# Final norm and stores of all rows moved ahead of the last expert block's output, whose rows are gathered, summed, normed and scattered afterwards

## The chip, the cores and the metric

One core of one Trainium2 chip runs the whole program in one launch. The metric is device time in microseconds (us), from the start of the program to its end. The time before is the median of three runs.

## The reference, cut to what matters

Two transformer blocks work on 1024 tokens of 1024 float32 features. The first is left out here: the change doesn't touch it. The second ends in a mixture of 32 experts, two per token, and a final norm:

```python
def second_block(x, ...):
    ...
    x = x + gate_a * mix
    h = rms_norm_2(x, norm2_g[l]) * (1.0 + scale_f) + shift_f
    x = x + gate_f * hierarchical_moe(h, ...)
    return rms_norm_2(x, final_g)

def rms_norm_2(x, g):                       # over the 1024 features of a token
    y = x * lax.rsqrt(jnp.mean(x * x, axis=-1, keepdims=True) + EPS)
    return y * g

# hierarchical_moe: each token goes to 2 of 32 experts (d_model 1024, hidden 512)
#   y[token] += gate[token, e] * ((silu(h @ w_gate[e]) * (h @ w_up[e])) @ w_down[e])
```

## The kernel before

**Expert blocks.** Tokens are sorted into blocks of 128 slots. Blocks 0 to 31 are the first 128 tokens of each expert. An expert with more tokens gets overflow blocks (32, 33, ...), whose number is known only on the chip; with these inputs there are four (32 to 35), so block 35 is the last. A slot without a token has the index 1024, which the bounds check of the indirect DMAs skips. `h4_dram` holds the inputs of the experts and `x3_dram` the residual stream, to which every block adds its gated output with an accumulating indirect DMA (a scatter, `scatter_rows`, line 838, on the GpSimd queue).

**One overflow block** (`overflow(b)` of each engine) streams twelve chunks of weights of 512 KB through a ring of twelve slots (`ring`, SyncE, line 595). ScalarE rounds each chunk to fp32r (`mH`, line 1338), VectorE makes the remainder (`mL`, line 2095), and TensorE forms each product from three fp32r matmuls (lines 2139, 2140, 2142). Eight chunks are gate and up, four are down. Between these two groups TensorE transposes the gathered inputs of the next block (2634) and the hidden rows (2639), which VectorE (2101, 2105, 2110) and ScalarE (1341, 1345) prepare. At chunk 6 of block b, the output of the block before it is taken from PSUM (banks 4 and 5): ScalarE weights it by slot (`slot_w`) into `ys[1]` (line 1331), GpSimd waits until VectorE has made all twelve remainders, copies the destination indices (904), multiplies by the gate row (`gate_rows`, line 832) and scatters (838).

**The loop around it** (`overflow_blocks`, lines 421 to 429) runs over all 15 possible overflow blocks on each engine, with an `If` on the count read from the chip: the eleven that don't exist are empty turns of compare and branch.

**After the last block** ScalarE takes its output from PSUM in two halves (1353), GpSimd gates them (832) and scatters them into `x3_dram` (838, `last_tok`). When that scatter has landed, SyncE loads all eight tiles of 128 rows back from `x3_dram` (602). For each tile ScalarE sums the squares (1358), VectorE forms mean plus epsilon (`variance`, 2117), GpSimd raises it to the power -0.5 (923), VectorE multiplies by it and by `final_row` (`finish`, 2122), and SyncE stores the tile to `out` (605). The program ends when all stores have landed.

Of the kernel before, what the change touches and what calls it, by code (L numbers as in the profile page):

```python
# [12 lines left out]
P = 128  # L13
# [22 lines left out]
    tr_lo sums_out sums2_out sums_in row_cols row_tr row_copied rows_out rows_here c_here mid_tr tr_mid v_mm pool_steps neg_out mb_in mask_done exp_done small_ready small_exp sq_out intra_out kt_mm kw_out st_mm c_ready hd_out cell_w ov_l last_y last_out m2_row m2_dst rows_known aff_ready halves_out affT_tr m1_xT_lo m1_hid m1_hT_lo if_lo v_odd if_mm pool_mm k_mm k_out s_mm  # L36
# [47 lines left out]
def build(nc, ctx, io, out, room):  # L84
# [159 lines left out]
    for name in SEMS.split():  # L244
# [6 lines left out]
        [("sq2", NT), ("sq2_2", NT), ("sq_final", NT)],  # L251
        [("var2", NT), ("var2_2", NT), ("var_final", NT)],
        [("rstd2", NT), ("rstd2_2", NT), ("rstd_final", NT)],
# [166 lines left out]

    def overflow_blocks(eng, overflow):
# [10 lines left out]
    one_rows = [ring[:, 2 * t, :] for t in range(6)] + [xz[:, 6, :], sg]  # L432
    two_rows = [ring[:, 2 * t + 1, :] for t in range(6)] + [xz[:, 7, :], hid]
    x_rows = [(mH, mL)[t // WSETS][:, t % WSETS, :].bitcast(F32) for t in range(NT)]
# [16 lines left out]
    def _(sp):  # L451
# [145 lines left out]
        overflow_blocks(sp, overflow)  # L597

        sp.wait_ge(S["last_out"], 16)  # L600
        for t in range(NT):
            sp.dma_start(x_rows[t], x3_tiles[:, t, :]).then_inc(x_in[t], 16)
        for t in range(NT):
            sp.wait_ge(S["final_done"], t + 1)
            sp.dma_start(out.rearrange("(t p) d -> p t d", p=P)[:, t, :], one_rows[t]).then_inc(x_in[t], 16)
# [5 lines left out]
    def _(pool):  # L611
# [279 lines left out]
        def overflow(b):  # L891
# [7 lines left out]
            pool.wait_ge(m2_out[1], 16 * (E2 // 2 - 1) + XS_PAST)  # L899
            pool.wait_ge(m2_out[0], 16 * b + 16 * (E2 // 2) + XS_PAST)  # L900
            settle(pool)
            pool.wait_ge(S["m2_lo"], 12 * b + 12 * E2 + 11 + past["m2_lo"])
            settle(pool)
            pool.tensor_copy(tok_out[0][:], row_of[:, bass.ds(b + (E2 - 1), 1)]).then_inc(S["m2_row"], 1)
            gate_rows(gated, ys[1], slice(0, D))
            pool.wait_ge(S["m2_row"], 2 * b + 3 * (E2 - 1) + 2)
            settle(pool)
# [3 lines left out]
        pool.wait_ge(m2_out[1], 16 * (E2 // 2 - 1) + XS_PAST)  # L911
        pool.wait_ge(m2_out[0], 16 * blocks + 16 * (E2 // 2) + XS_PAST)
        settle(pool)
        pool.tensor_copy(last_tok[:], row_of[:, bass.ds(blocks + (E2 - 1), 1)]).then_inc(S["m2_row"], 1)
# [3 lines left out]
        pool.wait_ge(S["m2_row"], 2 * blocks + 3 * (E2 - 1) + 3)  # L918
        settle(pool)
        scatter_rows(ys[0], last_tok).then_inc(S["last_out"], 16)  # L920
        for t in range(NT):
            pool.wait_ge(S["var_final"], t + 1 + past["var_final"])
            pool.tensor_tensor(stat[:, 10, t:t + 1], stat[:, 9, t:t + 1], neghalf[:, 0:1], ALU.pow).then_inc(S["rstd_final"], 1)
# [3 lines left out]
    def _(act):  # L927
# [395 lines left out]
        def overflow(b):  # L1323
            used, hi = past["m2_used"] + 12 * E2, past["m2_xT_hi"] + 2 * E2
            for c in range(12):
                if c == 6:
                    act.wait_ge(S["m2_used"], 12 * b + used)
# [1357 lines left out]
```

## Time and profile before

| | us |
|---|---|
| time before, median of three runs | 2220.2 |
| the three runs | 2221.27, 2218.15, 2220.2 |
| span of the profiled execution, first to last instruction | 2217.8 |
| last matmul ends | 2183.1 |
| last scatter into x3_dram issued | 2188.5 |
| first reload of x3_dram issued | 2193.5 |
| last tile normed | 2212.0 |

The profile gives no time of its own for the profiled execution beside the span, which is 2.4 us below the median of the runs. TensorE is busy for 91% of the span, VectorE for 76%, ScalarE for 57%, GpSimd for 21%. All times of rows are microseconds from the start of the span. A name with a "q" behind the engine (POOLq) is its instruction queue, in which branches and the issue of DMAs run.

### The profile page before, as it was taken

The numbers are of one execution on the slowest core, as the hardware profiler recorded it, in microseconds if no ns is written. First come the engines' busy times: TensorE is split into PE (matmuls) and PEld (weight loads), VectorE is DVE, ScalarE is ACT, GpSimd is POOL, SyncE is SP. The second block draws the span as 40 slices with busy tenths as digits, with TensorE's granted clock in tenths as the row PEclk, the third lists the DMA queues.
The fourth block names the chain that finished last, engine by engine and source line by source line (L and its number), as shares of the span: only waits on it lengthen the run. The fifth ranks groups of instructions, "written<-read, shape, count | busy, mean of one in ns | idle before, by whom it ended". The sixth has DMA issues, their size and how long they took to land.

```text
span 2217.8 us, 31469 instructions
## 1 busy us (share of the span) xinstructions
PE 2018.8 (91%) x9493; PEld 1669.2 (75%) x9493; DVE 1695.3 (76%) x1917; ACT 1257.1 (57%) x1478; POOL 470.0 (21%) x371
## 2 busy tenths in 40 slices
PE   3999999959999999999599998975999999999993
PEld 3888878747888887878477776864888888788872
DVE  5676765469999999999517455446999999999994
ACT  4311112108888878787515423214888888888874
POOL 2000001101001011110101450110444443334533
PEclk9999999959999999999799999987999999999997
DMA  9276844629999999999411103354999999999994
GB/s 346 89 250 223 270 169 158 218 76 349 387 381 385 382 378 389 380 387 382 161 39 48 48 20 117 123 206 152 386 388 375 382 379 378 365 376 382 342 363 162
DMA packets 236193, 598.33 MB, mean 270 GB/s; under 512 B 24513, under 2 KB 61653, under 8 KB 236125
## 3 DMA queue, kind: packets, MB, share of 16 engines
q1 hardware_dynamic: 209536, 524.35, 63.5%
q0 software_dynamic: 22928, 60.93, 9.4%
q10 hardware_dynamic: 3660, 12.17, 1.5%
q8 instruction: 39, 0.64, 0.1%
q14 instruction: 30, 0.24, 0.0%
HBM read 567.39 MB, written 51.43 MB: 279 GB/s over the span
## 4 chain that ended last, share of the span: by engine, by line
PE 63%; DMA 14%; DVE 10%; SPq 4%; issue 4%; ACT 3%; POOL 1%; DVEq 0%; ACTq 0%; POOLq 0%
PE ps L2139 19%; PE ps L2142 18%; PE ps L2140 18%; DMA ring<-in_w_expert_up 6%; DMA ring<-in_moe_w_down 6%; SPq L533 4%; DVE mL L1630 1%; PE ps L2267 1%; DMA ring<-in_ada_w 1%; PE ps L2562 1%; PE ps L2407 1%; DVE mL L2026 1%; DVE xz L1776 1%; PE ps L2232 1%; ACT mH L1276 1%
## 5 line engine op out<-in xcount | busy, mean ns | idle before, releaser
L2026 DVE TENSOR_TENSOR mL<-ring,mH 128x1024 fp32r<-128x1024 f32 x384 | 482.9, 1299 | 17.6 <-ACT mH L1276 17.0
L1630 DVE TENSOR_TENSOR mL<-ring,mH 128x1024 fp32r<-128x1024 f32 x384 | 455.4, 1221 | 31.6 <-ACT mH L1095 22.0
L1095 ACT ACTIVATE mH<-ring 128x1024 fp32r<-128x1024 f32 x384 | 402.3, 1063 | 96.2 <-PE ps L2142 64.6
L2139 PE MATMUL ps<-mH,xsH 128*128 128x512 f32 x1088 | 437.1, 402 | 7.8 <-DVE mL L2026 4.4
L1276 ACT ACTIVATE mH<-ring 128x1024 fp32r<-128x1024 f32 x384 | 397.6, 1057 | 57.8 <-DMA ring<-in_w_expert_up 24.0
L2142 PE MATMUL ps<-mH,xsL 128*128 128x512 f32 x1088 | 427.4, 393 | 0.0
L2140 PE MATMUL ps<-mL,xsH 128*128 128x512 f32 x1088 | 425.7, 391 | 0.0
L2139 PEld LDWEIGHTS ps<-mH,xsH 128*128 128x128 f32 x1088 | 205.9, 189 | 48.9 <-issue 7.3
L2142 PEld LDWEIGHTS ps<-mH,xsL 128*128 128x128 f32 x1088 | 205.3, 189 | 44.4
L2140 PEld LDWEIGHTS ps<-mL,xsH 128*128 128x128 f32 x1088 | 206.0, 189 | 39.7
L2139 PE MATMUL ps<-mH,hidH 128*128 128x512 f32 x544 | 216.3, 398 | 9.1 <-DVE hidL L1675 5.7
L832 POOL TENSOR_TENSOR xz<-xz,gate_ffn_row 128x340 f32<-128x340 f32 (+3 forms) x99 | 166.8, 1690 | 247.8 <-DVE mL L2026 210.2
L2140 PE MATMUL ps<-mL,hidH 128*128 128x512 f32 x544 | 212.3, 390 | 0.0
L2142 PE MATMUL ps<-mH,hidL 128*128 128x512 f32 x544 | 167.9, 390 | 0.0
L2139 PE MATMUL ps<-hH,wH 128*128 128x512 f32 x384 | 152.1, 396 | 3.7 <-DVE hL L1432 3.3
L2140 PE MATMUL ps<-hL,wH 128*128 128x512 f32 x384 | 150.4, 392 | 0.0
L2139 PEld LDWEIGHTS ps<-mH,hidH 128*128 128x128 f32 x544 | 102.2, 188 | 33.6 <-DVE mL L1630 8.8
L1376 DVE SCALAR_TENSOR_TENSOR acc<-ring,silu_c,acc 128x1024 f32<-128x1024 f32 x83 | 106.6, 1284 | 21.7 <-DMA ring<-in_ada_w 14.8
L2142 PE MATMUL ps<-hH,wL 128*128 128x512 f32 x384 | 122.9, 391 | 0.0
L2142 PEld LDWEIGHTS ps<-mH,hidL 128*128 128x128 f32 x544 | 102.2, 188 | 21.8
L2140 PEld LDWEIGHTS ps<-mL,hidH 128*128 128x128 f32 x544 | 102.4, 188 | 19.7
L703 POOL DMA_INDIRECT xz<-h_dram,tok_in x16 | 37.1, 2322 | 376.0 <-DVE tok_in L1640 376.0
(419 smaller groups left out, 3162.7 us busy)
## 6 DMA issues: line engine op xcount, KB each, us to landing
ring<-in_w_expert_gate SPq DMA_DIRECT2D x144, 512.0 KB, 12.7
ring<-in_w_expert_up SPq DMA_DIRECT2D x144, 512.0 KB, 12.8
ring<-in_w_expert_down SPq DMA_DIRECT2D x144, 512.0 KB, 13.0
ring<-in_moe_w_gate SPq DMA_DIRECT2D x128, 512.0 KB, 11.7
ring<-in_moe_w_up SPq DMA_DIRECT2D x128, 512.0 KB, 11.6
ring<-in_moe_w_down SPq DMA_DIRECT2D x128, 512.0 KB, 13.7
ring<-in_ada_w SPq DMA_DIRECT2D x96, 512.0 KB, 7.0
ring<-in_sc_w_in SPq DMA_DIRECT2D x24, 512.0 KB, 8.8
```

The costliest lines, as they stand in the source:

```text
L533: sp.dma_start(dst, src).then_inc(ring_in[s], 16)
L703: pool.indirect_dma_start(out=xs[r], out_offset=None, in_=h2_dram, in_offset=bass.IndirectOffsetOnAxis(ap=tok_in[r][:, 0:1], axis=0)).then ...
L832: pool.tensor_tensor(dst[:, at], src[:, at], gate_ffn_row[:, at], ALU.mult).then_inc(S["m2_row"], 1)
L1095: act.activation(mH[:, m % WSETS, :], ring[:, m % RING, :], ACT.Copy).then_inc(S["m1_hi"], 1)
L1276: act.activation(mH[:, wset, :], ring[:, slot, :], ACT.Copy).then_inc(S["m2_hi"], 1)
L1376: ins = dve.scalar_tensor_tensor(out=acc[:], in0=slot, scalar=silu_c[:, silu_col + k:silu_col + k + 1], in1=acc[:], op0=ALU.mult, op1=ALU.add)
L1630: dve.tensor_tensor(mL[:, m % WSETS, :], ring[:, m % RING, :], mH[:, m % WSETS, :].bitcast(F32), ALU.subtract).then_inc(S["m1_lo"], 1)
L1776: ins = dve.scalar_tensor_tensor(out=xz[:, i, back:T], in0=tA[:, 0:T - back], scalar=col("conv_w_2", 4 * (3 - back) + i), in1=xz[:, i, bac ...
L2026: dve.tensor_tensor(mL[:, wset, :], ring[:, slot, :], mH[:, wset, :].bitcast(F32), ALU.subtract).then_inc(S["m2_lo"], 1)
L2139: pe.matmul(o, high, rh, start=start, stop=False)
L2140: pe.matmul(o, high, rl, start=False, stop=False)
L2142: last = pe.matmul(o, low, rh, start=False, stop=stop)
```

## The change

The rows of all tiles are reloaded once the output of the last block but one has been scattered, into ring slots as VectorE frees them, and normed and stored without the last block's contribution. That contribution is handled apart, in `ys[0]`: GpSimd gathers its tokens' rows from `x3_dram`; VectorE takes the last block's output from PSUM, weighted and gated in one operation (`weigh`), and adds the gathered rows; the sum is normed as a ninth tile (sixth in order, `FINAL_ORDER`) and scattered over `out` when all eight stores have landed. In the overflow blocks, `weigh` on VectorE takes the place of ScalarE's copy and GpSimd's multiplication, and GpSimd no longer waits for VectorE's remainders before the scatter.

```diff
+    FINAL_ORDER = [0, 1, 2, 3, 4, NT, 5, 6, 7]
+    x_rows = [ring[:, t, :] for t in range(NT)]
+    sq_rows = [ring[:, NT + u, :] for u in range(RING - NT)]
+    last_rows, last_base = ys[0], xz[:, 7, :]
 # SyncE, after the overflow blocks
-        sp.wait_ge(S["last_out"], 16)
+        sp.wait_ge(m2_out[0], 16 * (E2 // 2) + XS_PAST)
+        sp.wait_ge(m2_out[1], 16 * blocks + 16 * (E2 // 2 - 1) + XS_PAST)
         for t in range(NT):
+            sp.wait_ge(S["m2_lo"], 12 * blocks + 12 * (E2 - 1) + t + 1 + past["m2_lo"])
             sp.dma_start(x_rows[t], x3_tiles[:, t, :]).then_inc(x_in[t], 16)
         for t in range(NT):
             sp.wait_ge(S["final_done"], t + 1)
-            sp.dma_start(out...[:, t, :], one_rows[t]).then_inc(x_in[t], 16)
+            sp.dma_start(out...[:, t, :], x_rows[t]).then_inc(x_in[t], 16)
 # GpSimd, overflow(b)
             pool.wait_ge(S["ov_y"], b + 1 + past["ov_y"])
-            pool.wait_ge(S["m2_lo"], 12 * b + 12 * E2 + 11 + past["m2_lo"])
-            pool.tensor_copy(tok_out[0][:], row_of[...]).then_inc(S["m2_row"], 1)
-            gate_rows(gated, ys[1], slice(0, D))
-            scatter_rows(gated, tok_out[0]).then_inc(m2_out[0], 16)
+            pool.tensor_copy(tok_out[1][:], row_of[...]).then_inc(S["m2_row"], 1)
+            scatter_rows(ys[1], tok_out[1]).then_inc(m2_out[1], 16)
 # GpSimd, after the overflow blocks
-        for half in range(2):
-            pool.wait_ge(S["last_y"], half + 1)
-            gate_rows(ys[0], ys[0], slice(512 * half, 512 * half + 512))
-        scatter_rows(ys[0], last_tok).then_inc(S["last_out"], 16)
-        for t in range(NT):
-            ... pow of tile t
+        pool.indirect_dma_start(out=last_base, in_=x3_dram, in_offset=last_tok, ...).then_inc(S["last_in"], 16)
+        for i in range(NT + 1):
+            ... pow of entry i
+        for t in range(NT):
+            pool.wait_ge(x_in[t], 64)
+        pool.wait_ge(S["last_done"], 1)
+        pool.indirect_dma_start(out=out, in_=last_rows, out_offset=last_tok, ...).then_inc(S["last_out"], 16)
+        pool.wait_ge(S["last_out"], 16)
 # ScalarE: its copy at chunk 6 of overflow(b) and the two halves after the blocks are removed
-        for t in range(NT):
-            act.wait_ge(x_in[t], 48)
-            act.activation(two_rows[t], x_rows[t], ACT.Square, accum_out=...)
+        act.wait_ge(S["m2_lo"], 12 * blocks + 12 * E2 + past["m2_lo"])
+        for i, t in enumerate(FINAL_ORDER):
+            act.wait_ge(x_in[t], 48) if t < NT else act.wait_ge(S["last_y"], 1)
+            act.activation(sq_rows[i % 4], x_rows[t] if t < NT else last_rows, ACT.Square, accum_out=...)
 # VectorE
+        def weigh(dst, block):
+            return dve.scalar_tensor_tensor(out=dst, in0=ps[:, 4:6, :], scalar=slot_w[:, bass.ds(block, 1)],
+                                            in1=gate_ffn_row, op0=ALU.mult, op1=ALU.mult)
         def overflow(b):
             for c in range(12):
+                if c == 6:
+                    dve.wait_ge(S["m2_used"], 12 * b + 12 * E2 + past["m2_used"])
+                    dve.wait_ge(m2_out[1], 16 * b + 16 * (E2 // 2 - 1) + XS_PAST)
+                    weigh(ys[1], b + (E2 - 1)).then_inc(S["ov_y"], 1)
+        def last_sum():
+            dve.wait_ge(S["m2_used"], 12 * blocks + 12 * E2 + past["m2_used"])
+            step(weigh(last_rows, blocks + (E2 - 1)))
+            dve.wait_ge(S["last_in"], 16)
+            dve.tensor_tensor(last_rows, last_rows, last_base, ALU.add).then_inc(S["last_y"], 1)
-        for t in range(NT):
-            variance(t)
-            if t:
-                finish(t - 1)
-        finish(NT - 1)
+        for i, t in enumerate(FINAL_ORDER):
+            if t == NT:
+                last_sum()
+            variance(i)
+            if i:
+                finish(i - 1)
+        finish(NT)
```

## Rows read from the trace of the kernel before

**Rows 1.** Timeline of TensorE: start us, us, engine line operation; the last matmuls.
```profile
2182.01 0.39 PE L2139 MATMUL ps<-mH,hidH 128*128 128x512 f32 x1
2182.24 0.39 PE L2140 MATMUL ps<-mL,hidH 128*128 128x512 f32 x1
2182.47 0.61 PE L2142 MATMUL ps<-mH,hidL 128*128 128x512 f32 x2
```

**Rows 2.** Timeline of GpSimd after the last block; idle before a row in brackets.
```profile
2178.03 1.61 POOL L838 DMA_INDIRECT x_dram<-xz,tok_out  x1 [0.89 <-POOL xz L832]
2184.99 0.18 POOL L914 COPY last_tok<-row_of 128x1 uint32 x1 [5.36 <-DMA x_dram<-xz,tok_out]
2185.14 2.48 POOL L832 TENSOR_TENSOR xz<-xz,gate_ffn_row 128x512 f32<-128x512 f32 x2
2188.51 1.60 POOL L838 DMA_INDIRECT x_dram<-xz,last_tok  x1 [0.90 <-POOL xz L832]
```

**Rows 3.** Timeline of SyncE's queue: reloads, then stores.
```profile
2193.53 2.75 SPq L602 DMA_DIRECT2D mH<-x_dram  x6
...
2210.87 1.53 SPq L605 DMA_DIRECT2D out<-xz  x2
```

**Rows 4.** Timeline of ScalarE: end of the blocks, then the squares.
```profile
2176.78 1.10 ACT L1345 ACTIVATE xsH<-ps 128x512 fp32r<-128x512 f32 x2
2183.30 1.26 ACT L1353 ACTIVATE xz<-ps,slot_w 128x512 f32<-128x512 f32 x2 [5.42 <-PE ps L2142]
2196.86 1.06 ACT L1358 ACTIVATE ring<-mH 128x1024 f32<-128x1024 f32 x1 [12.30 <-DMA mH<-x_dram]
...
2200.62 1.06 ACT L1358 ACTIVATE ring<-mH 128x1024 f32<-128x1024 f32 x1 [0.89 <-DMA mH<-x_dram]
...
2201.90 1.06 ACT L1358 ACTIVATE ring<-mH 128x1024 f32<-128x1024 f32 x1
```

**Rows 5.** Timeline of VectorE: norms of the last tiles.
```profile
2206.57 1.28 DVE L2122 SCALAR_TENSOR_TENSOR ring<-mH,stat,final_row 128x1024 f32<-128x1024 f32 x1 [0.38 <-POOL stat L923]
...
2207.84 1.27 DVE L2122 SCALAR_TENSOR_TENSOR ring<-mH,stat,final_row 128x1024 f32<-128x1024 f32 x1
...
2209.55 2.48 DVE L2122 SCALAR_TENSOR_TENSOR xz<-mL,stat,final_row 128x1024 f32<-128x1024 f32 x2 [0.38 <-POOL stat L923]
```

**Rows 6.** DMA issues: size, median us from issue to landing; last row whole trace, others the end.
```profile
mH<-x_dram SPq DMA_DIRECT2D x6, 512.0 KB, 6.6
...
mL<-x_dram SPq DMA_DIRECT2D x2, 512.0 KB, 10.1
out<-xz SPq DMA_DIRECT2D x2, 512.0 KB, 5.3
...
x_dram<-xz,last_tok POOLq DMA_INDIRECT x1, 5.0
...
x_dram<-xt POOLq DMA_DIRECT2D x16, 512.0 KB, 2.9
```

**Rows 7.** DMA issues of four narrow windows: 2193.5, 2159.4, 2161.3 and 2124.2 us.
```profile
mH<-x_dram SPq DMA_DIRECT2D x1, 512.0 KB, 3.3
...
x_dram<-xz,tok_out POOLq DMA_INDIRECT x1, 6.0
...
xz<-h_dram,otok POOLq DMA_INDIRECT x1, 4.2
...
xz<-h_dram,otok POOLq DMA_INDIRECT x1, 7.9
```

**Rows 8.** Branches of the loop over overflow blocks: count, ns min/median/max, first and last start.
```profile
L427 ACTq COMPARE_BRANCH  x15: 39/50/55, 2100.8 to 2182.6; - x15
...
L427 POOLq COMPARE_BRANCH  x15: 39/50/55, 2108.2 to 2184.3; - x15
```

**Rows 9.** Timeline of VectorE in overflow blocks 32 and 35.
```profile
2103.80 15.09 DVE L2095 TENSOR_TENSOR mL<-ring,mH 128x1024 fp32r<-128x1024 f32 x12
2118.81 0.74 DVE L2101 TENSOR_TENSOR xz<-xz,ps 128x256 f32<-128x256 f32 x2
...
2160.04 6.91 DVE L2095 TENSOR_TENSOR mL<-ring,mH 128x1024 fp32r<-128x1024 f32 x6
2167.30 3.50 DVE L2095 TENSOR_TENSOR mL<-ring,mH 128x1024 fp32r<-128x1024 f32 x3 [0.35 <-ACT mH L1338]
2171.27 3.50 DVE L2095 TENSOR_TENSOR mL<-ring,mH 128x1024 fp32r<-128x1024 f32 x3 [0.48 <-ACT mH L1338]
2175.21 0.75 DVE L2101 TENSOR_TENSOR xz<-xz,ps 128x256 f32<-128x256 f32 x2 [0.44 <-PE ps L2142]
```

**Rows 10.** Line 1652 of the first block's experts: count, ns min/median/max, first and last start.
```profile
L1652 DVE SCALAR_TENSOR_TENSOR xz<-ps,slot_gate,gate_ffn_row x16: 1273/1274/1278, 541.8 to 1064.3; 128x1024 f32<-128x1024 f32 x16
```

**Rows 11.** Timeline: VectorE's first remainder of block 32; GpSimd's copy and scatter there.
```profile
2103.80 1.88 DVE L2095 TENSOR_TENSOR mL<-ring,mH 128x1024 fp32r<-128x1024 f32 x1
...
2118.01 0.92 POOL L904 COPY tok_out<-row_of 128x1 uint32 x1 [7.26 <-DVE mL L2095]
...
2122.28 1.60 POOL L838 DMA_INDIRECT x_dram<-xz,tok_out  x1 [1.01 <-issue]
```

More of the change, by code:

```diff
@@ L419, in m2_steps, with stat_of @@
             body(s // 2, s % 2)
+    FINAL_ORDER = [0, 1, 2, 3, 4, NT, 5, 6, 7]
+    def stat_of(i):
+        return [stat[:, 8 + n, i:i + 1] if i < NT else stat[:, 11, n:n + 1] for n in range(3)]
     def overflow_blocks(eng, overflow):
@@ L604, in _ @@
             sp.wait_ge(S["final_done"], t + 1)
-            sp.dma_start(out.rearrange("(t p) d -> p t d", p=P)[:, t, :], one_rows[t]).then_inc(x_in[t], 16)
+            sp.dma_start(out.rearrange("(t p) d -> p t d", p=P)[:, t, :], x_rows[t]).then_inc(x_in[t], 16)
         for t in range(NT):
@@ new lines, in _ @@
+        for i in range(NT + 1):
+            pool.wait_ge(S["var_final"], i + 1 + past["var_final"])
+            own = stat_of(i)
+            pool.tensor_tensor(own[2], own[1], neghalf[:, 0:1], ALU.pow).then_inc(S["rstd_final"], 1)
+        for t in range(NT):
+            pool.wait_ge(x_in[t], 64)
+        pool.wait_ge(S["last_done"], 1)
+        pool.indirect_dma_start(out=out, in_=last_rows, in_offset=None,
+                                out_offset=bass.IndirectOffsetOnAxis(ap=last_tok[:, 0:1], axis=0),
+                                bounds_check=T - 1, oob_is_err=False).then_inc(S["last_out"], 16)
@@ L2087, in _ @@
         m2_steps(dve, m2_step)
+        def weigh(dst, block):
+            return dve.scalar_tensor_tensor(out=dst.rearrange("p (a b) -> p a b", a=2), in0=ps[:, 4:6, :],
+                                            scalar=slot_w[:, bass.ds(block, 1)],
+                                            in1=gate_ffn_row[:].rearrange("p (a b) -> p a b", a=2),
+                                            op0=ALU.mult, op1=ALU.mult)
         def overflow(b):
@@ L2111, in overflow, with variance, finish @@
                                   part.bitcast(F32), ALU.subtract).then_inc(S["m2_xT_lo"], 1)
-        overflow_blocks(dve, overflow)
-        def variance(t):
-            dve.wait_ge(S["sq_final"], t + 1 + past["sq_final"])
-            dve.tensor_scalar(stat[:, 9, t:t + 1], stat[:, 8, t:t + 1], 1.0 / D, EPS, ALU.mult,
-                              ALU.add).then_inc(S["var_final"], 1)
-        def finish(t):
-            dve.wait_ge(S["rstd_final"], t + 1 + past["rstd_final"])
-            dve.scalar_tensor_tensor(out=one_rows[t], in0=x_rows[t], scalar=stat[:, 10, t:t + 1], in1=final_row[:],
-                                     op0=ALU.mult, op1=ALU.mult).then_inc(S["final_done"], 1)
-        dve.wait_ge(S["final_in"], 16)
-        for t in range(NT):
-            variance(t)
-            if t:
-                finish(t - 1)
-        finish(NT - 1)
+        blocks = overflow_blocks(dve, overflow)
+        def last_sum():
+            dve.wait_ge(S["m2_used"], 12 * blocks + 12 * E2 + past["m2_used"])
+            settle(dve)
+            dve.wait_ge(m2_out[0], 16 * (E2 // 2) + XS_PAST)
+            step(weigh(last_rows, blocks + (E2 - 1)))
+            dve.wait_ge(S["last_in"], 16)
+            dve.tensor_tensor(last_rows, last_rows, last_base, ALU.add).then_inc(S["last_y"], 1)
+        def variance(i):
+            own = stat_of(i)
+            dve.wait_ge(S["sq_final"], i + 1 + past["sq_final"])
+            dve.tensor_scalar(own[1], own[0], 1.0 / D, EPS, ALU.mult, ALU.add).then_inc(S["var_final"], 1)
+        def finish(i):
+            t = FINAL_ORDER[i]
+            own, rows = stat_of(i), x_rows[t] if t < NT else last_rows
+            dve.wait_ge(S["rstd_final"], i + 1 + past["rstd_final"])
+            dve.scalar_tensor_tensor(out=rows, in0=rows, scalar=own[2], in1=final_row[:], op0=ALU.mult, op1=ALU.mult
+                                     ).then_inc(S["final_done" if t < NT else "last_done"], 1)
+        dve.wait_ge(S["final_in"], 16)
+        for i, t in enumerate(FINAL_ORDER):
[5 more added lines that the diff above has]
+        finish(NT)
     @block.tensor
```

59 lines of the change are left out of this document (26 added, 33 removed).

## The prediction

> **What bounds the kernel now.** I read the page's chain of work that ended last for the whole, then one timeline per engine after 2090 us, then the landings of DMAs. Up to 2183.1 us the chain is TensorE's and the change only touches its overflow blocks. The tail from the last matmul [rows 1] to the end of the span at 2217.8 is 34.7 us in which nothing is multiplied. The reader should see it as a relay. ScalarE takes the product (two halves, 1.26), GpSimd, held by earlier work until 2184.99, gates it (2.48) and issues the scatter 0.90 later at 2188.51 [rows 2, 4]; this lands after 5.0 [rows 6], and the first reload goes out at 2193.53 [rows 3]. That is 10.4 us from matmul to reload. The first tile lands 3.3 later [rows 7]. Then squares, powers and norms follow each other, and the last norm ends at 2212.03 [rows 5]; its store is issued at once, lands 5.3 later [rows 3, 6], and 0.4 later the span ends.
>
> Two more things matter. The norm pipeline isn't bound by ScalarE, whose squares go 1.28 apart [rows 4]: VectorE's `finish` starts 1.27, then 1.71 after the last one, in turn [rows 5], since every second power waits on GpSimd. So a tile costs 1.49. And after the last real block each engine walks through eleven empty turns: ScalarE's last product ends at 2177.88 and its last turn branches at 2182.6, GpSimd goes from its scatter at 2178.03 to 2184.3 [rows 2, 4, 8]. With the instructions that follow, ScalarE is free at about 2183.0 and GpSimd about 6.8 us after its last scatter.
>
> **The overflow blocks.** `weigh` doesn't occur in this stage, but line 1652 is the same operation with the same shapes and operands in PSUM and SBUF: 1.274 us [rows 10]. Two such in a row start 1.20 apart (2.48 for two [rows 5]), so it lengthens VectorE's stream by 1.20. In block 32 VectorE works through twelve remainders without a gap and goes straight into the hidden rows that TensorE waits for [rows 9]: here 1.2 is added to the path. In blocks 33 to 35 the same stream has gaps of 0.35, 0.48 and 0.44, 1.27 in all [rows 9]. They hide the 1.20, the more so as ScalarE loses its copy of 1.1 us in front of chunk 6, so the rounded chunk is there earlier. I take nothing for these three; if the cover is gone it is 1.2 each, 3.6. What ScalarE and GpSimd lose (the copy, a gate multiplication and a wait) hides behind other work now and gives nothing back. So the last matmul moves from 2183.1 to **2184.3**, and ScalarE is free from its turns at 2183.0 + 1.2 = 2184.2.
>
> **The reloads.** The scatter of block 34 used to go out at 2178.03. Now `weigh` in block 35 starts after six remainders, at 2166.95 + 1.2 = 2168.1, and ends at 2169.4. GpSimd copies the indices; such a copy took 0.92 beside VectorE's remainders [rows 11], and after it 0.9 pass until the DMA [rows 2]. The scatter starts at 2171.3, lands 6.0 later as its like did [rows 7], and the first reload goes out at 2177.4. SyncE's own turns are long over by then. The tiles land from 2180.7 on (3.3, 5.0, 7.1 after the first issue by the starts of the first three squares [rows 4], the last after some 13.4, which is 10.1 from its own issue [rows 6]). The waits on `m2_lo` cost nothing: the last ring slot needed is free at about 2172. So at 2184.3 two or more tiles are there and the others stay ahead of ScalarE by 1 to 3 us: it's not the reloads but ScalarE's empty turns that release the first square, 12.6 us sooner than at 2196.86. **No square falls in the last block's matmuls**; only the reloads do.
>
> **The norms.** Squares at 2184.3, 2185.6, 2186.8, 2188.1 and 2189.4. `finish(0)` follows `variance(1)`, at 2186.95; then 1.71, 1.27, 1.71: `finish(3)` runs from 2191.6 to 2192.85. Here the order is written out: `last_sum` comes next, with everything of VectorE behind it. Product and gather are long ready (GpSimd: scatter at 2171.3, turns until 2178.1, gather issued at 2180, landed in 4.2 alone to 7.9 beside streaming [rows 7], by 2188). `weigh` 1.25 and its own completion 0.1, add 1.2: 2195.4. ScalarE has stood idle since 2190.7; its sixth square ends at 2196.7. `variance(5)`, then `finish(4)` at 2196.8, and four more at steps of 1.71, 1.27, 1.71, 1.2: the last starts at 2202.7 and ends at **2203.9**, 8.1 us before the old 2212.03. Of the 12.6 gained at the first square the detour through `last_sum` takes 3.9 (`finish(4)` at 2196.8 instead of 2192.9) and the ninth row 1.5; 1.0 comes back since the second and third tile no longer wait for their loads.
>
> **The end.** New behind the last norm is the chain store, wait, scatter. The store: 5.3 for the last two before [rows 6], with reloads and stores back to back; alone a store of that size took 2.9 and a reload 3.3 [rows 6, 7]. After `last_sum` there is a gap of 5 us in the norms, and the stores drain, so I take 3.3 (bounds 2.9 and 5.3): landed at 2207.3. Then 0.9 from release to issue (0.3 to 1.0), 2208.2. Scatters to `x3_dram` took 5.0, this very list of rows, to 6.1; a gather of the kind, which moves rows without adding, 4.2. A plain write of rows isn't shown. I take 4.5 (bounds 4.0 and 6.1): 2212.7. With 0.4 the span ends at **2213.1**, 4.7 us sooner. On the median that is 2220.2 - 4.7 = **2215.5**.
>
> **Rivals.**
>
> *The stores stay slow.* The last store lands after 5.3 and the scatter after 6.1. For it: these are what the rows of the tail show. Against: those stores ran behind 4 MB of reloads. It gives +2.0 + 1.6: 2219.1, no change.
>
> *GpSimd's scatter is held up by VectorE.* The scatter of block 34 moves from a time when VectorE is nearly through into its unbroken stream. If it couldn't be issued until that stream ends, at 2176.2 instead of 2171.3, the reloads would start 4.9 later, the third tile would land at 2189.4 instead of 2184.5, and its square, due at 2186.8, and all behind it would be 2.6 late: 2218.1. Against: a scatter issued just as VectorE's stream began took 1.60 like those beside an idle VectorE [rows 2, 11]. The Trainium skill speaks for this in SBUF — State Buffer, section "SBUF: two separate sides", box "The 'DVE blocks DMA' trap": while VectorE runs an operation that holds the port pair it shares with GpSimd, GpSimd can't write the descriptors of its DMAs. By that rule, if the remainders count as such, the result is this rival's; by the rows it is the sum above.
>
> *VectorE becomes the bound of every overflow block.* The gaps sum to 1.27 against 1.20 added, a margin of 0.07. If they can't be used, and a remainder is stretched from 1.14 to 1.88 by GpSimd's copy, as the first one of block 32 was [rows 11], blocks 33 to 35 cost 1.94 each: +5.8, 2221.3, slower than before. The sign turns at 4.7 / 3 = 1.6 us per block, a loss of 0.2% needs 3.0. Against: the copy is 128x1 and ends at once when the port is free.
>
> **How the numbers follow.** About 0.2%, 4.4 us, is what can be told from no change here; the line lies at 2215.8, just beside my sum. The forecast as worked out, give or take 1.5: 0.52, a little over half of it below the line. Slow stores and scatter, whole or in part: 0.20. VectorE in the way of the scatter: 0.08. VectorE as the bound: 0.08. Better than the sum (store 2.9, scatter 4.0, release 0.3, which is 1.5 less: 2214.0): 0.12, nearly all faster. That makes faster 0.43, same 0.51, slower 0.06. The range goes from 2213.0 (the good bounds and 1.0 for a cheaper block 32) to 2221.0; the likeliest case's own is 2214.0 to 2217.0.
>
> **What would show it.** Step by step: remainders and `weigh` of block 32 end at about 2120.1 and the blocks after it stay 18.8 apart; first reload near 2177.4; first square at 2184.3 with idle time ended by no DMA; a gap of 4.6 on ScalarE after five squares; last norm near 2204; last store landing within 3.5; last scatter landing within 5. A first square later than 2186, a block longer than 19.5, or more than 10 us from the last norm to the end would make the prediction wrong.

## The result, and the profile after

The changed kernel takes 2224.57 us (2222.48 to 2227.02, 18 runs) against 2219.65 us (2216.39 to 2221.61, 18 runs) beside it. The ratio is 1.0022, with an interval of 1.0015 to 1.0029: slower by 4.9 us, where 4.7 us faster was forecast. A second set of runs of the same kernel (`e11`, below) gave 1.0021 (1.0012 to 1.0030). The time lies outside the range given, 2213.0 to 2221.0.

The profiled execution took 2223.24 us with a span of 2221.6 us, 3.8 us longer than the span of before. The granted clock is 0.958 over the whole. The blocks ahead of the change run 0.44 us earlier than in the execution of before, which is chance.

VectorE of the changed kernel in block 32, and again around block 35 (timeline: start, us, engine, line, operation):

```profile
2103.36 8.28 DVE L2112 TENSOR_TENSOR mL<-ring,mH 128x1024 fp32r<-128x1024 f32 x6
2111.56 1.27 DVE L2097 SCALAR_TENSOR_TENSOR xz<-ps,slot_w,gate_ffn_row 128x1024 f32<-128x1024 f32 x1
2112.76 6.89 DVE L2112 TENSOR_TENSOR mL<-ring,mH 128x1024 fp32r<-128x1024 f32 x6
...
2167.67 1.28 DVE L2097 SCALAR_TENSOR_TENSOR xz<-ps,slot_w,gate_ffn_row 128x1024 f32<-128x1024 f32 x1
2168.86 6.90 DVE L2112 TENSOR_TENSOR mL<-ring,mH 128x1024 fp32r<-128x1024 f32 x6
```

`weigh` takes 1.27 and stands between six remainders and six. From one block's copy of `otok` to the next's, block 32 lasts 19.66 us (before 18.46), blocks 33 and 34 last 18.79 and 18.88 (before 18.79 and 18.83). So the work in the blocks costs what was forecast: 1.2 once, nothing after. But look at the second half of block 35 beside [rows 9]: the gap of 0.48 that stood in it is gone, the six remainders follow each other without one.

GpSimd of the changed kernel, from block 35 to its last instruction:

```profile
2169.39 6.41 POOL L912 COPY tok_out<-row_of 128x1 uint32 x1 [6.39 <-DVE xz L2097]
2176.68 1.59 POOL L848 DMA_INDIRECT x_dram<-xz,tok_out  x1 [0.88 <-POOL tok_out L912]
2183.47 0.18 POOL L918 COPY last_tok<-row_of 128x1 uint32 x1 [5.19 <-issue]
2184.63 1.07 POOL L924 DMA_INDIRECT xz<-x_dram,last_tok  x1 [0.98 <-POOL last_tok L918]
...
2203.27 2.04 POOL L930 TENSOR_TENSOR stat<-stat,neghalf 128x1 f32<-128x1 f32 x2 [0.94 <-DVE stat L2143]
2211.02 1.05 POOL L934 DMA_INDIRECT out<-xz,last_tok  x1 [5.72 <-DMA out<-ring]
```

The first row is the surprise of the blocks: a copy of 128 words that takes 6.41 us. It starts at 2169.39 and ends at 2175.80; VectorE's six remainders end at 2175.76. The same copy took 6.40 in block 33 and 6.41 in block 34. The scatter behind it is 5.4 us later than forecast (2176.68 against 2171.3), and so is everything that waits for its landing.

SyncE's queue, then ScalarE's squares and VectorE's last norms:

```profile
2183.09 3.92 SPq L612 DMA_DIRECT2D ring<-x_dram  x8
2190.31 17.36 SPq L615 DMA_DIRECT2D out<-ring  x8
```

```profile
2186.49 1.06 ACT L1365 ACTIVATE ring<-ring 128x1024 f32<-128x1024 f32 x1 [7.78 <-DMA ring<-x_dram]
...
2190.34 1.06 ACT L1365 ACTIVATE ring<-ring 128x1024 f32<-128x1024 f32 x1 [1.44 <-DMA ring<-x_dram]
...
2198.87 1.06 ACT L1365 ACTIVATE ring<-xz 128x1024 f32<-128x1024 f32 x1 [4.14 <-DVE xz L2138]
```

```profile
2196.24 1.28 DVE L2097 SCALAR_TENSOR_TENSOR xz<-ps,slot_w,gate_ffn_row 128x1024 f32<-128x1024 f32 x1
2197.56 1.22 DVE L2138 TENSOR_TENSOR xz<-xz 128x1024 f32<-128x1024 f32 x1
...
2204.83 2.48 DVE L2149 SCALAR_TENSOR_TENSOR ring<-ring,stat,final_row 128x1024 f32<-128x1024 f32 x2 [0.38 <-POOL stat L930]
```

The last matmul ends at 2183.87 and the first reload goes out at 2183.09: only 0.8 us of what the change was to put beside the matmuls lies beside them. The idle time before the first square is ended by a load, and so is that before the third, fourth and fifth. The last norm ends at 2207.30, 4.7 before [rows 5], not 8.1. That is still sooner than before. What turns the sign comes later: the last store is issued at 2207.33 and lands 2.7 later, GpSimd's scatter starts at 2211.02 and lands after 2.9, at 2213.95, and yet the span ends at 2221.60.
```
kernel  engine   start us   lasts us
before  SyncE    2217.60    0.01
before  GpSimd   2209.22    8.02
after   SyncE    2210.29    0.01
after   GpSimd   2214.11    7.26
```

GpSimd's record ends the span of the changed kernel. In the kernel before it starts beside the last power (ended 2210.04), ends at 2217.24, 7.2 us after it, and lies hidden behind the last store with 0.4 us to spare.

The miss in the profiled execution, 2221.6 against 2213.1 forecast, is made up so: last norm +3.4, last store's landing -0.6 (2.7 for 3.3), release of the scatter +0.1, scatter's landing -1.6 (2.9 for 4.5), and from that landing to the end +7.2 (7.6 for 0.4). Sum +8.5.

### The profile page after: what moved, and what is told of

Its sections match the earlier page's. It is cut to its first block and busy times, and to the rows that moved or that the text cites. A ratio compares the mean times of both kernels' runs of the same rounds, so it can differ in the third digit from the quotient of the medians.

```text
span 2221.6 us, 31489 instructions
## 1 busy us (share of the span) xinstructions
PE 2014.1 (91%) x9493; PEld 1662.1 (75%) x9493; DVE 1700.7 (77%) x1925; ACT 1253.9 (56%) x1474; POOL 480.6 (22%) x367
## 5 line engine op out<-in xcount | busy, mean ns | idle before, releaser
L842 POOL TENSOR_TENSOR xz<-xz,gate_ffn_row 128x340 f32<-128x340 f32 (+1 forms) x93 | 155.3, 1674 | 249.1 <-DVE mL L2033 210.4
```

The lines of the kernel that those rows point to most:

```text
L842: pool.tensor_tensor(dst[:, at], src[:, at], gate_ffn_row[:, at], ALU.mult).then_inc(S["m2_row"], 1)
```

## The experiments

Each ratio is to the kernel before, run on the same chip beside it; its 95% interval is in brackets. The differences in us are those of the medians, unless a span is named.

### The end: is it GpSimd's last instruction?

`e3` is the kernel before with one thing added: after its last power GpSimd waits for all output stores.

```diff
             pool.tensor_tensor(stat[:, 10, t:t + 1], stat[:, 9, t:t + 1], neghalf[:, 0:1], ALU.pow)...
+        for t in range(NT):
+            pool.wait_ge(x_in[t], 64)
```

> Change of the kernel before: GpSimd, whose last power ends at 2210.0, also waits for the landing of all eight stores, at 2217.4; nothing else. Theory C (a drain of 7.2 us behind GpSimd's last instruction, hidden in the kernel before because it ends 0.4 us ahead of the last store's landing): 7 us slower than the kernel before. Rival D (the long drain belongs to the scatter into the output): no change, at most 0.3 us.

Measured: 2227.50 against 2220.72, 1.0028 (1.0017 to 1.0040), slower by 6.8 us. SyncE's stores of this kernel go out as in [rows 3], 0.7 later:

```profile
2201.22 8.97 SPq L605 DMA_DIRECT2D out<-ring  x6
2211.59 1.53 SPq L605 DMA_DIRECT2D out<-xz  x2
```

SyncE is through at 2218.42. GpSimd's DRAIN starts at 2218.44, lasts 7.18, and ends at 2225.62, 0.2 before the span's end at 2225.85. Nothing else was added, and the medians of the timed runs show 6.8. So GpSimd needs some 7.2 us after its last instruction or wait, and a kernel that lets it wait for the last transfer pays that.

`e2` takes the other way, in the changed kernel: SyncE, not GpSimd, waits for the landing of the last scatter.

```diff
-        pool.wait_ge(S["last_out"], 16)
 # SyncE, after its waits for the stores
+        sp.wait_ge(S["last_out"], 16)
```

> Change of the kernel after: GpSimd issues the last scatter and has nothing more to wait for; SyncE waits for its landing. Theory C (GpSimd takes some 7.2 us to drain once its last instruction is done, whatever that is): the drain starts 1.9 us sooner, beside the scatter's flight, 1.9 us faster. Rival D (the drain waits for the landing of the outstanding scatter and its length follows from that): no change, or a drain of over 9 us.

Measured: 2222.06 against 2220.72, 1.0008 (0.9999 to 1.0017), where the changed kernel has 1.0022 and 1.0021: 3.1 us less by the ratios, 3.6 by the medians, where 1.9 was expected. The two intervals together leave about 2.5 us either way, so 1.9 is not excluded.

```profile
2214.78 1.05 POOL L935 DMA_INDIRECT out<-xz,last_tok  x1 [5.72 <-DMA out<-ring]
```

The issue ends at 2215.83 and DRAIN at 2223.10, 7.27 later; the span ends 8.6 after the start of this row, in the changed kernel 10.6, so this trace shows 2.0. The landing of 2.9 us now lies beside the DRAIN, which is no longer for it. What is left, 7.3 from the end of the issue on, stands at the end of every version here in which GpSimd issues the last scatter.

### The scatter of block 34: its copy, or the port?

`e1` gives the copy of the indices to VectorE, in front of `weigh`; GpSimd only scatters.

```diff
 # GpSimd, overflow(b)
-            pool.tensor_copy(tok_out[1][:], row_of[:, bass.ds(b + (E2 - 1), 1)]).then_inc(S["m2_row"], 1)
-            pool.wait_ge(S["m2_row"], b + 3 * (E2 - 1) + 1)
+            pool.wait_ge(S["m2_dst"], b + E2)
 # VectorE, c == 6
+                    dve.tensor_copy(tok_out[1][:], row_of[...]).then_inc(S["m2_dst"], 1)
                     weigh(ys[1], b + (E2 - 1)).then_inc(S["ov_y"], 1)
```

> Change of the kernel after: VectorE, not GpSimd, copies the index column just ahead of weigh. Theory A (GpSimd's 128x1 copy waits 6.4 us for the port that VectorE's unbroken stream of remainders holds): the scatter of block 34 goes out at about 2170.2 instead of 2176.7, the first reload at 2176.4 instead of 2183.1, the first square at 2184 instead of 2186.5 (then ScalarE's empty turns hold it), the squares after it no longer wait for loads, the last norm ends at 2203.6 instead of 2207.3: 3.7 us faster than the kernel after. Rival B (the descriptors of the scatter are what VectorE's stream holds back, so the scatter waits with or without a copy): scatter still at 2176, no gain.

Measured: 2225.18 against 2220.72, 1.0020 (1.0011 to 1.0029): nothing gained. The copy is gone and the scatter itself has become long. VectorE, then GpSimd, of this kernel in block 35:

```profile
2171.12 1.27 DVE L2096 SCALAR_TENSOR_TENSOR xz<-ps,slot_w,gate_ffn_row 128x1024 f32<-128x1024 f32 x1
2172.31 6.89 DVE L2112 TENSOR_TENSOR mL<-ring,mH 128x1024 fp32r<-128x1024 f32 x6
```

```profile
2173.55 7.11 POOL L848 DMA_INDIRECT x_dram<-xz,tok_out  x1 [7.16 <-issue]
```

It starts 1.24 us into the remainders, which end at 2179.20, and it ends 1.46 after them, about what the whole instruction takes elsewhere (1.59). In blocks 32, 33 and 34 of this kernel the scatter took 5.73, 2.56 and 6.92: in block 33 it did not wait for the last remainder. The first reload leaves at 2185.49, 1.8 before the last matmul's end at 2187.28.

`e10` is `e1` with a hole in VectorE's stream: the remainder of chunk 7 computes a single column.

```diff
+                n = 1 if c == 7 else D
-                dve.tensor_tensor(mL[:, c % WSETS, :], ring[:, c, :], mH[:, c % WSETS, :].bitcast(F32),
+                dve.tensor_tensor(mL[:, c % WSETS, 0:n], ring[:, c, 0:n], mH[:, c % WSETS, 0:n].bitcast(F32),
```

> e1_copy_dve with VectorE's remainder of chunk 7 of each overflow block cut to one column (the other 1023 are stale, so the output is not the reference's): VectorE has about 1 us without work from 1.1 us after weigh on. Theory B (VectorE's unbroken stream of operations with two SBUF inputs keeps GpSimd from writing the descriptors of its scatter, and one gap is enough to let it in): the scatter of block 34 takes 1.6 to 3 us on GpSimd instead of 7.1, the first reload goes out 4 to 5 us sooner against the last matmul, and no square of the first five waits over 1 us for a load; kernel 2.5 to 4 us faster than e1_copy_dve. Rival N (the scatter is slow for its 128 rows and the weights streaming beside it): still 7 us.

Measured: 2219.84 against 2220.19, 0.9997 (0.9988 to 1.0006), 4.8 us less than `e1` by the differences. Not all of it is the scatter's: the last norm ends 19.8 after the last matmul, in `e1` 22.5, which is 2.7; block 32 is 1.1 shorter by the missing remainder (18.66 for 19.77); the rest may be the clock, which falls in `e1` (see `e7`) and not here. VectorE and GpSimd in block 35:

```profile
2169.09 2.57 DVE L2113 TENSOR_TENSOR mL<-ring,mH 128x1024 fp32r<-128x1024 f32 x3
2172.27 3.50 DVE L2113 TENSOR_TENSOR mL<-ring,mH 128x1024 fp32r<-128x1024 f32 x3 [0.61 <-ACT mH L1344]
```

```profile
2170.34 1.58 POOL L848 DMA_INDIRECT x_dram<-xz,tok_out  x1 [7.16 <-issue]
```

The same instruction takes 1.58 where a piece of the stream is missing: it starts before the next remainder does (2170.44). In block 34 it starts 0.1 into a whole remainder, takes 2.58, and ends 1.46 after that remainder, where the hole is. In block 32 it starts behind the hole, takes 4.96 and again ends 1.45 after the last remainder. In block 35 the scatter's rows and the weights that stream beside it are those of `e1`, so they aren't what made it slow there. The first reload leaves at 2176.76, 7.3 ahead of the last matmul's end at 2184.05, and no square waits for a load:

```profile
2184.64 1.06 ACT L1364 ACTIVATE ring<-ring 128x1024 f32<-128x1024 f32 x1 [5.76 <-issue]
...
2185.69 1.04 ACT L1364 ACTIVATE ring<-ring 128x1024 f32<-128x1024 f32 x1
```

This is the machine of the prediction: the square is released 5.76 after ScalarE's last product (2178.88) by nothing but its own empty turns. A hole was needed for that, so the kernel that computes everything doesn't have it.

The Trainium skill's rule that the prediction set against its rows (SBUF — State Buffer, "SBUF: two separate sides", the box "The 'DVE blocks DMA' trap") speaks of VectorE's operations in a 2-port mode. Block 35 behaves as it says, 7.11 with the stream and 1.58 with the hole, though the remainders are `tensor_tensor`. The same page, under "Who interferes with whom", infers that `tensor_tensor` doesn't hold up the writing of descriptors, since it takes only the read side of the pair. These runs show that it can hold up the issue of an indirect DMA; but that issue also takes its 128 indices from SBUF, and no run tells that reading from the writing of descriptors, so they don't refute the inference. The page also has the pair locked for one instruction; the traces agree with that in part.

Behind `weigh`, GpSimd's copy or scatter waited for the last of the remainders in 33 of 42 blocks (eleven kernels: all with `weigh` but `e10`), all eleven blocks 35 among them. In the other nine it got in when the one remainder that was running had ended (`e9`, block 33: 2.56, in a stream without a gap). And in front of `weigh` it always got in. The changed kernel, blocks 32 and 35:

```profile
2106.91 1.64 POOL L848 DMA_INDIRECT x_dram<-xz,tok_out  x1 [0.89 <-POOL xz L842]
2108.85 1.46 POOL L904 DMA_INDIRECT xz<-h_dram,otok  x1 [0.30 <-issue]
...
2161.71 1.29 POOL L904 DMA_INDIRECT xz<-h_dram,otok  x1 [2.11 <-DVE otok L2105]
```

VectorE's six remainders follow each other without a gap around all three (from 2103.36 and from 2160.85). So a hole lets the scatter in, but a stream without one doesn't always keep it out; what decides is open.

`e5` leaves out the scatters of the outputs of blocks 31 to 34, and the waits for them, so that the reloads wait for free ring slots alone. It shows the most that earlier reloads could bring.

```diff
-            scatter_rows(ys[1], tok_out[1]).then_inc(m2_out[1], 16)
```

> Change of the kernel after: the scatters of blocks 31 to 34 into x3_dram are left out (their contributions are missing from the output), and with them the waits on them; the index copies stay. The reloads then need only the ring slots. Theory A (late reloads hold the norms back by 3.4 us, and behind them stand ScalarE's eleven empty turns): reloads out by about 2172, all tiles there before ScalarE is free; first square 5.1 to 5.3 us after ScalarE's last product of block 35, five squares 1.28 apart with no wait for a DMA, last norm 19.6 us after the first square; 3 to 3.7 us faster than the kernel after. Rival E (something else than the reloads holds the first square, the turns being shorter or longer): first square as late as before, or earlier than 5.1 us after the last product.

Measured: 2222.30 against 2220.36, 1.0009 (1.0000 to 1.0018), 2.9 us less than the changed kernel by the ratios. The first reload leaves at 2167.57, the first square starts 5.8 after ScalarE's last product, and five squares follow 1.04 apart. The last norm ends 19.9 after the last matmul, in the changed kernel 23.4. Hence 3.5 us of the tail are the price of the late reloads, and so of the late scatter. (Its profiled execution has a fall of the clock in block 33, see `e7`; the tail is measured from the last matmul and so is free of it.)

### Both, and the order of the last rows

`e4` is `e1` and `e2` together.

> The first two edits together. Theories A and C: 3.7 + 1.9 = 5.6 us faster than the kernel after, 2219.0 against 2219.65 of the kernel before, no difference from it that can be measured. If B or D hold, one of the two parts is missing.

Measured: 2221.70 against 2220.72, 1.0007 (0.9998 to 1.0016), as `e2` alone: the copy's new place is worth nothing, as `e1` had said. The forecast above counted on more.

`e6` is `e4` with the detour moved: the tiles are squared and normed in the order 0 to 7, the last block's rows come ninth, and `last_sum` stands behind six finished tiles.

```diff
-    FINAL_ORDER = [0, 1, 2, 3, 4, NT, 5, 6, 7]
+    FINAL_ORDER = [0, 1, 2, 3, 4, 5, 6, 7, NT]
-            if t == NT:
+            if i == 7:
                 last_sum()
```

> e4_both with two edits: the last block's rows come last of the nine, and last_sum runs on VectorE ahead of the eighth variance. Theory F (last_sum with a wait on both sides costs 3.9 us in the sixth place, and as VectorE work alone 2.5; with the ninth rows last the last store lands under their norm): the gap of 4.4 us on ScalarE goes, the last norm ends about 1.3 us sooner against the first square, and the scatter follows it by 1 us plus what is left of the last store's flight instead of 3.6: 3 to 4 us faster than e4_both, and so 2 to 3 us faster than the kernel before. Rival G (the last norm is bound by the DMA transfers, not by the order): no gain over e4_both.

Measured: 2219.62 against 2220.36, 0.9998 (0.9989 to 1.0007), about 2 us less than `e4` (3 to 4 were expected, and the two traces show 3.0 from the last matmul on). The last norm is now that of the rows that no plain store takes away, so the last store is issued at 2203.54 and lands beside it; the scatter starts 2.7 after the last norm's end, not 3.7. The squares of tiles 5 to 7 no longer stand behind VectorE's sum either.

### The blocks

`e7` is the kernel before with the blocks' part of the change alone: `weigh` on VectorE, GpSimd's scatter right after it, no early reloads, norms as before.

```diff
-            pool.wait_ge(S["m2_lo"], 12 * b + 12 * E2 + 11 + past["m2_lo"])
-            gate_rows(gated, ys[1], slice(0, D))
-            scatter_rows(gated, tok_out[0]).then_inc(m2_out[0], 16)
+            scatter_rows(ys[1], tok_out[1]).then_inc(m2_out[1], 16)
 # ScalarE's copy at c == 6 is removed; VectorE, at c == 6, has the operation of weigh
+                    dve.scalar_tensor_tensor(out=ys[1]..., in0=ps[:, 4:6, :], scalar=slot_w[...],
+                                             in1=gate_ffn_row..., op0=ALU.mult, op1=ALU.mult)
```

> Change of the kernel before: only the overflow blocks' part of the change (weigh on VectorE at chunk 6, no gating and no wait for the remainders on GpSimd); the end is that of the kernel before. Theory H (1.2 us more in block 32, nothing in the three blocks after it): last matmul 1.3 us later against the start of block 32, whole kernel 0.3 to 1.3 us slower, since GpSimd was the last to be ready for the last output by 1.0. Rival I (VectorE is the bound of each block now): 4 to 5 us slower.

Measured: 2222.83 against 2220.36, 1.0009 (1.0000 to 1.0018), slower by 2.5, between the two theories. In its profiled execution block 32 lasts 20.00 and block 33 no less than 21.07, which neither had. The reason shows in TensorE's rows. `e2` has it too; there it is plainest. Busy times in block 33, in the changed kernel for the 6.6 us after the stall of block 32, in `e2` for the stall, 6.6 us of the slow stretch and 12 us behind it; columns: window, its length, then busy us (and count) of PE, PEld, DVE, ACT, POOL, then granted clock, DMA share, GB/s; first the changed kernel, then `e2`:

```profile
2121.60:2128.20 6.60, 6.60 (x29) 5.46 (x30) 6.45 (x9) 6.28 (x8) 1.98 (x2) 1.00 0.95 332
```

```profile
2117.70:2121.60 3.90, 2.25 (x13) 1.53 (x11) 3.90 (x5) 0.00 (x0) 1.60 (x1) 1.00 1.00 392
...
2123.40:2130.00 6.60, 6.60 (x17) 5.27 (x18) 5.02 (x8) 4.60 (x6) 1.27 (x1) 0.55 0.90 319
2130.00:2142.00 12.00, 12.00 (x55) 9.92 (x54) 11.32 (x10) 8.87 (x9) 2.42 (x2) 1.00 0.93 329
```

The granted clock falls from 2.4 to 1.2 GHz for 6.8 us, and 17 matmuls run where the changed kernel has 29. Block 33 lasts 21.57 in place of 18.8. What TensorE did before: it stood idle in front of its second group of transposes, in `e2`, in the changed kernel and in `e6` (both of which kept their clock):

```profile
2121.82 0.77 PE L2668 MATMUL ps<-ident,xz 128*128 128x128 f32 x4 [1.87 <-DVE xz L2118]
```

```profile
2120.03 0.77 PE L2668 MATMUL ps<-ident,xz 128*128 128x128 f32 x4 [1.17 <-DVE xz L2118]
```

```profile
2119.79 0.77 PE L2668 MATMUL ps<-ident,xz 128*128 128x128 f32 x4 [2.06 <-DVE xz L2118]
```

In the kernel before, this wait is 0.27 us long and its one profiled execution keeps the clock. Of ten profiled executions with `weigh` in block 32, five show a fall there (`e1`, `e2`, `e5`, `e7`, `e8`, for 3.4 to 6.8 us) and five none (2.06 idle in `e6`, 0.79 in `e7`, so the length of this wait doesn't part them). Of the four without `weigh` there (before, `e3`, `e9`, `e12`) none shows one behind block 32. Five of ten against none of four makes `weigh` the likely cause and doesn't show it. The profiled execution of the changed kernel is one without, so its 3.8 us hold nothing of this; the timed runs, 4.9 slower, may.

`e8` takes the loop over the 15 overflow blocks apart into 4 and 11, so that the eleven empty turns are skipped by one branch (on the base of `e6`).

```diff
-            with eng.Fori(0, NOVF) as b:
+        for first, count in ((0, 4), (4, NOVF)):
+            with eng.If(blocks > first):
+                with eng.Fori(first, count) as b:
```

> e6_order with the loop over overflow blocks cut in two, turns 0 to 3 and 4 to 14, the second behind one branch of its own, so that the eleven empty turns are skipped on each engine. Theory J (the turns hold ScalarE for 5 us behind its last product, but the reloads land no earlier): ScalarE waits for the first tile instead of walking turns, first square at most 0.3 us sooner; gather some 1 us sooner at most; 0 to 0.5 us faster than e6_order. Rival K (the turns are what releases the first square): 2 us or more faster.

Measured: 2219.55 against 2220.36, 0.9998 (0.9989 to 1.0007), the value of `e6`. ScalarE's idle time before the first square (6.68) is ended by a load, as in `e6`: with the reloads late it is they, not the turns, that release the squares.

`e9` treats block 32 as before (ScalarE copies, GpSimd gates, no `weigh` on VectorE), the others as in `e6`.

```diff
 # all engines
+            overflow(0)
-            with eng.Fori(0, NOVF) as b:
+            with eng.Fori(1, NOVF) as b:
 # GpSimd
+            if static(b):
+                pool.wait_ge(S["m2_lo"], 12 * E2 + 11 + past["m2_lo"])
+                gate_rows(ys[1], ys[1], slice(0, D))
 # VectorE; ScalarE's copy at c == 6 is back for this block
+                    if not static(b):
                         weigh(ys[1], b + (E2 - 1)).then_inc(S["ov_y"], 1)
```

> e6_order with the first overflow block (32) written out ahead of the loop and in the old way: ScalarE weights the output of block 31, GpSimd gates it after the remainders; VectorE gets no weigh there. Theory L (in block 32, where VectorE sets the pace, weigh lengthens TensorE's idle stretch by 1.2 us, and in 5 of 8 profiled executions with it the granted clock then fell to 0.5 for 3.4 or 6.8 us, which made block 33 up to 2.8 us longer; in none of the two without): block 32 is 1.2 us shorter than in e6_order, the clock stays at 1.00 behind it, the timed runs are 1.2 to 3.5 us faster than e6_order, so 2.5 to 4 us faster than the kernel before. Rival M (the clock falls without regard to weigh): falls here too, 1.2 us at most.

Measured: 2218.05 against 2220.19, 0.9986 (0.9977 to 0.9995). Block 32 is at 18.52, but its later scatter now holds up VectorE in block 33:

```profile
2129.00 0.15 DVE L2120 COPY tok_out<-row_of 128x1 uint32 x1 [1.29 <-DMA x_dram<-xz,tok_out]
```

That block lasts 19.96, the clock falls behind it for 3.4 us, at 2140.1, and block 34 lasts 20.37. The stall had moved, and in this execution the fall of the clock with it.

`e12` is `e9`, and gives block 32's scatter rows and indices of their own (`gated`, `last_tok`), so that block 33 doesn't wait for its landing; block 33 is written out ahead of the loop too.

```diff
-                gate_rows(ys[1], ys[1], slice(0, D))
-            scatter_rows(ys[1], tok_out[1]).then_inc(m2_out[1], 16)
+                gate_rows(gated, ys[1], slice(0, D))
+            scatter_rows(gated if first else ys[1], last_tok if first else tok_out[1]).then_inc(m2_out[1], 16)
```

> e9_first_old with a buffer and an index column of its own for block 32's scatter, and block 33 written out too, so that its weigh waits for GpSimd's gating of block 32 alone and not for that scatter's landing (in e9_first_old VectorE stood 1.3 us idle there, TensorE's idle stretch in block 33 grew, and the clock fell to 0.5 for 3.4 us behind it, 2.7 us in blocks 33 and 34 together). Theory L (a clock fall follows where a block's idle stretch of TensorE is lengthened by some 1.2 us): blocks 33 and 34 back at 18.8 to 18.9 us each and no fall; 1.2 to 2.7 us faster than e9_first_old, so 0.20% to 0.26% faster than the kernel before. Rival M (falls come without regard to it): no more than 1.2 us faster, and a fall at some block in about half of the executions.

Measured: 2216.91 against 2219.86, 0.9989 (0.9980 to 0.9998), 2.9 us less than before and 7.9 less than the changed kernel by the differences: a version that beats both, the one before by an interval that just leaves out 1. The blocks last 18.52, 18.62 and 18.65, with no fall of the clock. It isn't to be told from `e9`. The scatter of its block 34 still takes 7.11:

```profile
2168.22 7.11 POOL L852 DMA_INDIRECT x_dram<-xz,tok_out  x1 [7.16 <-issue]
...
2206.61 1.05 POOL L942 DMA_INDIRECT out<-xz,last_tok  x1 [4.43 <-DMA out<-ring]
```

`e11` is the changed kernel again, on the chip and beside the runs of `e9` and `e10`.

> The kernel after, unchanged, on the same chip as the two above, as the base of their differences and as one more profiled execution of block 32 with weigh. By theory L its clock falls behind block 32 in more than half of the executions; the ratio to the kernel before should be that of the first comparison, 1.0022 within its interval.

Measured: 2225.03 against 2220.19, 1.0021 (1.0012 to 1.0030); in its profiled execution the last matmul ends at 2183.17, the first reload leaves at 2182.25 and the span ends at 2220.67. No fall of the clock here either.

## Why the prediction was wrong

**The overflow blocks: right in the profiled execution.** 1.2 in block 32, nothing in blocks 33 to 35; the timed runs of `e7`, which has this part alone, are 2.5 slower. The rival in which VectorE bounds every block didn't come: the copy of 6.4 us didn't stretch the remainders, since it waited for them. Its price was misread as well: [rows 11] has no copy beside the remainder of 1.88. What ran beside it was GpSimd's gate multiplication, three instructions from 2100.98 to 2106.45, the first row here (the kernel before):

```profile
2100.98 5.47 POOL L832 TENSOR_TENSOR xz<-xz,gate_ffn_row 128x344 f32<-128x344 f32 x3 [6.93 <-ACT xz L1289]
2107.35 1.64 POOL L838 DMA_INDIRECT x_dram<-xz,tok_out  x1 [0.90 <-POOL xz L832]
2109.29 1.46 POOL L894 DMA_INDIRECT xz<-h_dram,otok  x1 [0.30 <-issue]
```

What no step of the prediction had is TensorE's longer idle time there and the clock that it can cost: 21.57 for block 33 in `e2`. The clock in the blocks was never looked at; the one trace of before has no fall there.

**The reloads: the step "GpSimd copies the indices; such a copy took 0.92 beside VectorE's remainders" failed.** First reload 2183.09 for 2177.4. The row it rested on [rows 11] says the opposite when its end is worked out: the copy started at 2118.01 and ended at 2118.93, and VectorE's twelve remainders ended at 2103.80 + 15.09 = 2118.89. It had not run beside them; it had waited for the last one. The second piece of evidence, a scatter of 1.60 at 2122.28 "just as VectorE's stream began", began first:

```profile
2122.41 4.63 DVE L2095 TENSOR_TENSOR mL<-ring,mH 128x1024 fp32r<-128x1024 f32 x4
```

VectorE's row starts 0.13 after it. Neither row spoke against the rival "GpSimd's scatter is held up by VectorE", which was given 0.08. Rows that did speak against it were in the same trace and weren't used: the scatter and the gather at 2107.35 and 2109.29 above lie inside the twelve remainders and took 1.64 and 1.46. They would have supported the choice that turned out wrong: in block 35, behind `weigh`, GpSimd waited for the last remainder in every kernel with a full stream. That rival's own numbers fit: scatter after the stream, at 2176.2 (measured 2176.68), some 2.6 on the last norm (measured 3.4, 3.5 by `e5`).

**The norms: right in their working, late in their start.** "ScalarE's empty turns release the first square" is false of the changed kernel, where a load does, and true of `e5` and `e10`, with 5.8 from the end of the last product to the first square, against 5.2 in the forecast. The detour through `last_sum` is there as forecast: `finish(4)` waits for weigh, add and a square (idle 4.14 on ScalarE), and `e6` wins about 2 us by moving it.

**The end: the step "With 0.4 the span ends" failed, and it is the largest.** The 0.4 was read where SyncE's landing ended last, and carried over to an end where GpSimd is last. GpSimd's closing 7.2 us were in the trace of before, hidden; no term of the sum asked when each engine is done. `e3` shows their price by itself, 6.8. Against them the store (2.7 for 3.3) and the scatter (2.9 for 4.5) came out better than taken, inside or below their bounds.

With the two failed steps put right (+7.2 and +3.4) and the landings as measured, the sum is that of the profiled execution. That leaves 1.1 us between the difference of the spans (3.8) and that of the medians (4.9). The profiled execution of the changed kernel is 1.3 below its median, inside the spread of its runs (2222.48 to 2227.02), so 1.1 can be chance. The clock is a candidate for that spread: its mean over 29 runs of the changed kernel (with `e11`) is 0.9549 and over 104 runs of before 0.9559, and the fall in `e2`, half the clock for 6.8 of 2223 us, would lower one run's mean by 0.0015. In the changed kernel longer runs are those at a lower clock (correlation -0.41), in the kernel before they aren't (0.10). That fits a fall in about two of three runs at 2 to 3 us each; no trace of a timed run shows it, so it is argued and not shown.

Open as well: why the clock falls in one execution and not in another of nearly the same stall, and what GpSimd does in its DRAIN. That its length hardly changes is shown (7.18 to 7.42 from the last instruction or wait in every kernel here), and no more. Open too is what lets GpSimd in between two remainders in one place and not in another.

## What to carry to other kernels

Before work is moved behind the last store, write down for every engine when its last instruction and its last wait end, and what its end costs; a wait for the last stores at GpSimd's end cost 7 us here, and moving the wait for the last scatter from GpSimd to SyncE gave 2 to 3.6 back. A row's duration is a price only if its overlap was checked: where a GpSimd row ends within 0.1 us of VectorE's stream, it waited for it, and where it started first it says nothing of waiting. And a stream without gaps is no free cover: with VectorE's last gap filled, GpSimd was shut out for 6 us, and 1.2 us more of idle TensorE was in some executions followed by a fall of the clock that cost up to 2.8 more.

## What the runs showed of the hardware

- GpSimd's closing DRAIN ends 7.2 us after its last instruction or wait (7.26 in the changed kernel, 7.20 before, 7.18 in `e3`).
- A GpSimd copy of 128x1 took 6.41 us, and an indirect DMA's issue 7.11 for 1.58, beside six back-to-back remainders with both inputs in SBUF, in block 35; in one or the other form this wait stands there in all eleven kernels with `weigh` and no hole. In nine of their other 31 blocks GpSimd got in after one remainder, and the gathers in the first half of each block took 1.2 to 1.5 beside the same kind of stream.
- TensorE's granted clock fell to 1.2 GHz for 3.4 to 6.8 us in five of ten executions with `weigh` in block 32, and in none of four without it there (one of these, `e9`, has its fall behind block 33). The length of the wait for the last transposes didn't decide it: 0.79 (`e7`) and 1.87 (`e2`) with a fall, 1.17 (changed kernel) and 2.06 (`e6`) without, 0.27 before.
- An indirect write of the last block's rows to `out`, without adding, landed in 2.9 us; the same rows added to `x3_dram` took 5.0 in the kernel before and 5.2 in `e3`.
